# Gate and up weights in pieces of 16 KB: four chunks of 2 MB an expert in place of eight of 1 MB

## The reference

```python
logits = x @ w_router + b_router
top_logit, top_e = top_k(logits, 4)            # 4 of 32 experts for each token
gate = softmax(top_logit)
# for each expert e, for the rows xb routed to it:
gu = xb @ w_gu[e] + b_gu[e]                    # 1024 -> 2048
g, u = split(gu, 2)
g = minimum(g, 7.0); u = clip(u, -7.0, 7.0)
y = ((u + 1.0) * g * sigmoid(1.702 * g)) @ w_down[e] + b_down[e]   # 1024 -> 1024
# y times its gate is summed into the token's row
```

## Time and profile before

| | |
|---|---|
| median of three runs | 1621.77 us |
| the profiled execution's own time | 1619.32 us |
| its span, first to last instruction | 1617.6 us |
| TensorE busy | 1380.0 us, 85% |
| VectorE / ScalarE / GpSimd busy | 25% / 17% / 18% |
| mean rate of the DMAs over the span | 338 GB/s |
| mean granted TensorE clock | 0.913 of full speed |
| chain that ended last, by engine | PE 54%, DMA 34% |
| DMA packets | 110,253 |

### The profile page before, as it was taken

The page is one execution under the profiler, slowest core; times in us unless marked ns, Lnnn a source line. Parts: engine busy times, 40 slices in busy tenths (PEclk is TensorE's granted clock), DMA queues, the critical chain, the costliest instruction groups (busy, mean ns, idle before and its releaser), DMA issues.

```text
span 1617.6 us, 21742 instructions
## 1 busy us (share of the span) xinstructions
PE 1380.0 (85%) x8299; PEld 723.4 (45%) x8299; DVE 398.6 (25%) x759; ACT 282.7 (17%) x496; POOL 293.9 (18%) x288
## 2 busy tenths in 40 slices
PE   4799977788899578999999898899999889986667
PEld 2457753353699444444434443343444334332222
DVE  2358235553122532121111102111111211110103
ACT  1213444343233200111000101100010110000000
POOL 1336523222276010101001110100111010010000
PEclk9899989898999778998999899999989999977777
DMA  9665778776744637999999999999999999999974
GB/s 331 263 259 174 263 276 291 257 288 216 278 157 149 274 131 270 420 420 421 421 421 420 421 420 420 420 415 419 413 420 418 411 420 394 422 419 419 420 294 166
DMA packets 110253, 547.08 MB, mean 338 GB/s; under 512 B 14576, under 2 KB 14696, under 8 KB 57603
## 3 DMA queue, kind: packets, MB, share of 16 engines
q1 hardware_dynamic: 92704, 496.93, 77.0%
q0 software_dynamic: 16544, 45.72, 7.7%
q10 hardware_dynamic: 898, 3.01, 0.5%
HBM read 540.35 MB, written 13.63 MB: 342 GB/s over the span
## 4 chain that ended last, share of the span: by engine, by line
PE 54%; DMA 34%; DVE 5%; ACT 3%; SPq 2%; issue 1%; POOL 1%; ACTq 0%; POOLq 0%; DVEq 0%
PE PS L1583 48%; DMA wide<-in_w_down 19%; DMA wide<-in_w_gu 10%; PE PS L1761 4%; DMA ring<-in_w_in 3%; SPq L533 1%; DMA arena<-in_g_norm 1%; DMA ring<-in_cache_sb_v 1%; POOL WL L619 1%; PE PS L1937 1%; SPq L542 1%; ACT WL L770 0%; PE PS L1956 0%; PE PS L1737 0%; DMA ring<-in_w_ada 0%
## 5 line engine op out<-in xcount | busy, mean ns | idle before, releaser
L1583 PE MATMUL PS<-wide,arena 128*32 128x256 f32 (+2 forms) x4416 | 786.2, 512 | 101.8 <-DMA wide<-in_w_down 52.2
L1583 PEld LDWEIGHTS PS<-wide,arena 128*32 128x32 f32 (+2 forms) x4416 | 314.2, 141 | 546.2 <-issue 384.6
L687 POOL DMA_INDIRECT choice_rows<-arena,rows_of x31 | 31.8, 1026 | 693.7 <-ACT arena L1037 447.5
L619 POOL TENSOR_TENSOR WL<-ring,WL 128x1024 fp32r<-128x1024 f32 x48 | 119.6, 2506 | 132.9 <-ACT WL L770 132.8
L1583 PE MATMUL PS<-WH,WL 128*128 128x288 f32 x768 | 106.0, 299 | 6.3 <-DVEq L1340 3.1
L1583 PEld LDWEIGHTS PS<-WH,WL 128*128 128x128 f32 x768 | 104.2, 190 | 10.2 <-DVEq L1340 3.4
L1494 DVE TENSOR_SCALAR arena<-PS 128x256 f32<-128x256 f32 (+1 forms) x23 | 12.2, 529 | 346.6 <-PE PS L1583 346.6
L1583 PE MATMUL PS<-WL,WH 128*128 128x512 f32 (+1 forms) x288 | 74.4, 421 | 12.2 <-POOL WL L619 6.7
L770 ACT ACTIVATE WL<-ring 128x1024 fp32r<-128x1024 f32 x56 | 58.1, 1055 | 149.7 <-DMA ring<-in_w_in 92.7
L1045 ACT ACTIVATE arena<-arena 128x256 f32<-128x256 f32 (+1 forms) x23 | 11.5, 500 | 367.8 <-DVEq L1495 367.8
L1583 PE MATMUL PS<-ring,arena 128*32 128x512 f32 x256 | 61.4, 656 | 16.8 <-DMA ring<-in_cache_sb_v 13.7
(11 more groups left out here) (280 smaller groups left out, 1120.5 us busy)
## 6 DMA issues: line engine op xcount, KB each, us to landing
wide<-in_w_gu SPq DMA_DIRECT2D x256, 1024.0 KB, 23.5
wide<-in_w_down SPq DMA_DIRECT2D x128, 1024.0 KB, 25.0
ring<-in_w_ada SPq DMA_DIRECT2D x24, 1024.0 KB, 7.1
ring<-in_w_in SPq DMA_DIRECT2D x20, 1024.0 KB, 7.9
ring<-in_cache_sb_k SPq DMA_DIRECT2D x32, 256.0 KB, 4.3
ring<-in_cache_sb_k POOLq DMA_DIRECT2D x32, 256.0 KB, 5.4
ring<-in_cache_sb_v SPq DMA_DIRECT2D x32, 256.0 KB, 4.3
ring<-in_cache_sb_v POOLq DMA_DIRECT2D x32, 256.0 KB, 4.8
```

What stands on the lines that cost most here:

```text
L619: pool.tensor_tensor(low, raw_half(h), high.bitcast(F32), ALU.subtract).then_inc(mix_low, 1)
L687: pool.indirect_dma_start(Y4.rearrange("t (h n) -> (t h) n", h=n), bass.IndirectOffsetOnAxis(ap=rows_of[:, at, 0:1], axis=0), YB[it % 2 if ...
L1583: return T.matmul(out, lhsT, rhs, start=start, stop=stop, skip_group_check=True)
```

## The change

Gate and up weights are cut differently. A partition now takes two neighbouring rows of `w_gu`, a piece of 16 KB, and a chunk is 2 MB and fills two slots: four chunks an expert. Partition p of chunk j holds rows 256j + 2p and 256j + 2p + 1. `gu_big` and `gu_few` wait for a chunk once, go through its two k-tiles, and count it in `chunks_used` once. The contraction's rows are thus dealt out in another order, so `turn_rows` takes every second column out of 256. An expert has 8 chunks in place of 12, and the counts `gu_used` and `dn_used` follow. The down chunks, the slots and their memory stay. Expert 0's gate-up chunk j waits until two ring items more are used, and the tail's read of `choice_rows` waits for chunk i in place of chunk 2i + 1, which is the same slots.

```diff
-EXP_CHUNKS = 12
+WIDE = 12
+EXP_CHUNKS = 8
...
-GU_CHUNKS, DN_CHUNKS = 8, 4
+GU_CHUNKS, DN_CHUNKS = 4, 4
...
-    return (it + 1) * EXP_CHUNKS + DN_CHUNKS + j + 1
+    return (it + 1) * EXP_CHUNKS + GU_CHUNKS - DN_CHUNKS + j + 1
...
-        w_gu = t["w_gu"][0].rearrange("e (k p) n -> e p k n", p=P)
+        w_gu = t["w_gu"][0].rearrange("e (k p two) n -> e p k (two n)", p=P, two=2)
...
+        def gu_slot(j):
+            return wide[:, 2 * j:2 * j + 2, :]
+
+        def dn_slot(j):
+            return wide[:, 2 * GU_CHUNKS + j, :]
...
-                        sp.wait_ge(used, min(NSTREAM - SLOTS + j + 1, NSTREAM))
+                        sp.wait_ge(used, min(NSTREAM - SLOTS + 2 * j + 2, NSTREAM))
...
-                    sp.dma_start(wide[:, j, :], src).then_inc(expert_in[j], 16)
+                    sp.dma_start(gu_slot(j).rearrange("p s n -> p (s n)"), src).then_inc(expert_in[j], 16)
...
-                sp.wait_ge(chunks_used, gu_used(NE - 1, 2 * i + 1))
+                sp.wait_ge(chunks_used, gu_used(NE - 1, i))
...
-                    last = T.transpose(PS[:, 6 + k // 4, (k % 4) * P:(k % 4 + 1) * P], rows[:, k * P:(k + 1) * P], ident)
+                    cols = rows[:, 2 * P * (k // 2):2 * P * (k // 2 + 1)]
+                    last = T.transpose(PS[:, 6 + k // 4, (k % 4) * P:(k % 4 + 1) * P], cols[:, k % 2::2], ident)
...
             def gu_big(it, j):
                 pe.wait_ge(expert_in[j], 16 * (it + 1))
-                w = c3(wide[:, j, :], 512)
-                for q in range(4):
-                    last = mm(PS[:, q, :], XT[:, j, :], w[:, q, :], j == 0, j == DT - 1)
+                for k in range(2 * j, 2 * j + 2):
+                    w = c3(gu_slot(j)[:, k % 2, :], 512)
+                    for q in range(4):
+                        last = mm(PS[:, q, :], XT[:, k, :], w[:, q, :], k == 0, k == DT - 1)
                 last.then_inc(chunks_used, 1)
...
             def gu_few(it, j, n):
                 pe.wait_ge(expert_in[j], 16 * (it + 1))
                 w, per = FF // n, DT // n
-                rows = c3(wide[:, j, :], FF)
-                for gu in range(2):
-                    for g in range(n):
-                        last = mm(PS[rows_of_group(g, n), gu, 0:w], XT[:, j % per, rows_of_group(j // per, n)],
-                                  rows[:, gu, w * g:w * g + w], False, j == DT - 1)
+                for k in range(2 * j, 2 * j + 2):
+                    rows = c3(gu_slot(j)[:, k % 2, :], FF)
+                    for gu in range(2):
+                        for g in range(n):
+                            last = mm(PS[rows_of_group(g, n), gu, 0:w], XT[:, k % per, rows_of_group(k // per, n)],
+                                      rows[:, gu, w * g:w * g + w], False, k == DT - 1)
                 last.then_inc(chunks_used, 1)
```

More of the change, by code:

```diff
@@ L162, in build @@
             XP = early("XP", [P, 4, DT, P], F32R)
-        wide = sb("wide", [P, EXP_CHUNKS, SLOTW])
+        wide = sb("wide", [P, WIDE, SLOTW])
         xT = sb("xT", [P, DT, NTOK])
@@ L541, in load_down @@
                     src = w_dn[bass.ds(e, 1), :, j, :].rearrange("a p n -> (a p) n")
-                    sp.dma_start(wide[:, GU_CHUNKS + j, :], src).then_inc(expert_in[GU_CHUNKS + j], 16)
+                    sp.dma_start(dn_slot(j), src).then_inc(expert_in[GU_CHUNKS + j], 16)
             def load_bias(it, e):
@@ L1960, in gu_big @@
                 pe.wait_ge(expert_in[j], 16 * (it + 1))
-                w = c3(wide[:, j, :], 512)
-                for q in range(4):
-                    last = mm(PS[:, q, :], XT[:, j, :], w[:, q, :], j == 0, j == DT - 1)
+                for k in range(2 * j, 2 * j + 2):
+                    w = c3(gu_slot(j)[:, k % 2, :], 512)
+                    for q in range(4):
+                        last = mm(PS[:, q, :], XT[:, k, :], w[:, q, :], k == 0, k == DT - 1)
                 last.then_inc(chunks_used, 1)
             def down_big(it, j):
-                pe.wait_ge(expert_in[8 + j], 16 * (it + 1))
-                w = c3(wide[:, 8 + j, :], D)
+                pe.wait_ge(expert_in[GU_CHUNKS + j], 16 * (it + 1))
+                w = c3(dn_slot(j), D)
                 for k in range(2 * j, 2 * j + 2):
@@ L1989, in gu_few @@
                 w, per = FF // n, DT // n
-                rows = c3(wide[:, j, :], FF)
-                for gu in range(2):
-                    for g in range(n):
-                        last = mm(PS[rows_of_group(g, n), gu, 0:w], XT[:, j % per, rows_of_group(j // per, n)],
-                                  rows[:, gu, w * g:w * g + w], False, j == DT - 1)
+                for k in range(2 * j, 2 * j + 2):
[4 more added lines that the diff above has]
+                                      rows[:, gu, w * g:w * g + w], False, k == DT - 1)
                 last.then_inc(chunks_used, 1)
             def down_few(it, j, n):
-                pe.wait_ge(expert_in[8 + j], 16 * (it + 1))
+                pe.wait_ge(expert_in[GU_CHUNKS + j], 16 * (it + 1))
                 w, per = D // n, DT // n
-                rows = c3(wide[:, 8 + j, :], D)
+                rows = c3(dn_slot(j), D)
                 for k in range(2 * j, 2 * j + 2):
```

## The result

The changed kernel took 1612.51 us in the median of six runs (1607.85 to 1614.43), the kernel before 1622.04 us (six runs). The ratio is 0.9948 with a 95% interval of 0.9929 to 0.9967: 8.4 us less (5.4 to 11.5). A second comparison gave 0.9959 (0.9945 to 0.9973). Together the change is worth about half a per cent.

What follows compares the result with a forecast made beforehand. The expert stage was taken as bound by the slowest DMA engine's time for its weight pieces. Terms -9.2 + 1.4 + 0.3 = -7.5 us gave 1611.8 for the profiled execution, 1614.3 for the median; range 1605 to 1623.

Steps and rivals of the forecast that it cites:

- the saving in the stream: Expert weight queue: 32 pieces and four semaphore writes fewer save 0.308 us an expert, 9.2 us over 30 experts.
- What bounds the stage: Expert stage: the slowest DMA engine's time for its share of 12 MB sets the pace, 31.31 us an expert.
- The price of a piece: Gate-up loads: one 16 KB piece beats two of 8 KB by 8.5 ns, middle of 7.1 and 9.9; bounds 0 and 16.3.
- the prediction's own correction: Piece times from the DMA view: divided by the queues' summed share, as packets overlap; 315.5 became 311.4 ns under load.
- B: Weight stream: the whole raw difference, 16.3 ns, is real because load disturbs packets, not bytes; -15.0 us, 1606.8; chance 0.18.
- The start of the stream: Expert 2's first chunk waits for two k-tiles of expert 1 in place of one: 1.4 us lost.
- Expert 0 and the release in pairs: Expert 0's later first chunk and slots freed one k-tile later both cost nothing, covered by slack and 19 to 28 us landings.
- Rival C: Big experts: slots freed in pairs let the slowest engine run dry, 27.4 us lost, 1641.7; chance 0.07.
- Strided transposes: Row transposes before the first expert: weight loads of 208 against 155 ns, eight on the chain, 0.3 us lost.
- The end: End of the expert stage: down chunks still end the chain, so 2 MB gate-up chunks cost nothing there.
- Rival A: Weight stream: a 16 KB piece costs two of 8 KB, so +0.6 us, 1622.4; chance 0.20 with gains up to half.
- the Trainium skill: Weight queue: its 2.0 us per DMA is not seen between queued chunks; joining pieces pays only to 256 bytes, so no gain.

Runs made afterwards that it cites:

- bias_twice: Changed kernel with each expert's 8 KB bias row fetched a second time into an unused partition of the same tile; 1624.37 us, ratio 1.0022 to the kernel before.
- bias_spread_2: Changed kernel with the bias row fetched by two DMAs of alternate 64-float runs, spread over the engines; 1614.22 us, ratio 0.9965 to the kernel before.
- gu_8k: Changed kernel with the same 2 MB gate-up chunks, each fetched as two 8 KB pieces a partition; 1620.64 us, ratio 1.0014 to the kernel before.

## Why the prediction was right, point by point

The forecast was 1614.3 us, 7.5 us less; measured were 8.4 us less in the first comparison (9.5 between the medians) and 0.0041 of 1620.6, 6.6 us, in the second. The forecast, not a rival, came true. That it came this near owes something to luck: the saving in the stream was put 2 us too high, and the two comparisons lie 1.8 us apart.

*What bounds the stage.* The pace of the slowest engine. bias_twice shows it: 8 KB on one engine cost 10 us, some sixteen times what a mean rate would make of them. The semaphore writes show the last engine 9.5 us behind the next by expert 30, and the bias row on it. The prediction left open what makes that engine slow. I then took the bias row for it, and bias_spread_2 showed that taking the row away is not enough; the reason is open.

*The price of a piece.* 8.5 ns for each piece less was put down, between 0 and 16.3. The runs gave 8 ns from 16 to 8 KB, 9 from 8 to 4 KB, 9 on the down weights. So the price was right to within 1 ns, but the way to it was not. The packets' own durations in the trace, 640 to 1540 us, are 315.4 ns in the mean for a piece of 8 KB before and 620.9 for one of 16 KB after. With the prediction's own correction (over 1.004) the latter is 618.4, where it had 612.9 to 615.7: load added more to a piece of 16 KB than it allowed for. And B's 16.3 ns came from setting pieces under load against tail pieces without it. The raw difference, both under load, is 2 x 315.4 - 620.9 = 9.9 ns, and the next packet of an engine begins 3 to 4 ns before the end of the one before, so each piece less also gives up one such overlap. The prediction's correction would leave 2 x 311.4 - 618.4 = 4.4 ns. The 8.5 was the middle of two options that both missed the load, and its fit with 8 to 9 is partly luck.

The sum of the term was too high, 0.308 us an expert against 0.23 to 0.26 measured. Of this 0.036 were four semaphore writes, of which gu_8k shows nothing (31.33 against 31.31), and the rest is no more than the spread of the paces. 30 x 0.24 = 7.2 us in place of 9.2.

*The start of the stream.* 1.4 us was put down, 1.5 to 1.7 measured between TensorE's first gate-up matmul of expert 1 and SyncE's issue. TensorE's first k-tiles of expert 1 run at a granted clock of 0.50 (626.93 to 628.90 us) and 0.53 (up to 630.70), about the lower level of 1.2 GHz, and those behind them at 1.00, so one k-tile more costs more there than the mean of 1.06 us. The first issue came at 630.77 and not at 629.3; 1.1 us of this come from the matmuls, which began later.

*Expert 0 and the release in pairs.* Nothing and nothing. Here a number of the text was wrong, though its conclusion held. I had doubled SyncE's longest wait of 3.2 us to 6.4. SyncE's waits of the changed kernel in 640 to 1540 us (total, times, longest), against the earlier trace rows:

```profile
SPq L540 <- PE PS L1590: 476.1, 116, 10.9
```

The longest is 10.9 us. The reserve of 18 to 28 us covers that too, and 23.4 us is still the median landing time of gate-up chunks in that stretch. Rival C would have needed a reserve under 4.9.

*Strided transposes.* The weight load of L1945 (L1937 before) went from 155 to 208 ns, the figure of L1956, as expected. The eight transposes on the chain took 1.96 us against 1.94 before, so the 0.3 us were not there.

*The end.* From the landing of the last chunk to the end of the span it is 35.8 us in both (1576.87 to 1612.7, 1581.85 to 1617.6).

*The sum.* -7.2 + 1.6 = -5.6 us by the paces, and the profiled executions differ by 4.9. The measured 6.6 to 8.4 us are 1 to 3 us more, and the intervals of the ratios, 2.3 us either side and more, allow that. Part of it is the start: the changed kernel's profiled execution reached expert 1's gate-up matmuls 1.1 us later. From there to the end of the span it is 991.8 us before and 985.8 and 985.0 in the two profiles of the changed kernel, 6.0 to 6.8 less.

*Rival A and the Trainium skill.* Rival A wanted 31.3 us an expert; it was 31.08. Making the pieces 16 KB paid 8 ns for each piece less, which is 1.3% of the time of a 16 KB piece and just above the noise of the kernel.

The prediction used two sections more widely than they are meant. The Trainium skill, "DMA: Bandwidth & Descriptors", section "Why small descriptors are slow", calls packetization, the joining of consecutive descriptors into one packet, worth it only up to 256 bytes. This change makes the piece itself larger, so it does not follow from there that it gains nothing, and no run here tests packetization. The Trainium skill, "DMA: Bandwidth & Descriptors", section "Anatomy of one DMA", gives its fit of 2.0 us plus bytes / 436e3 for DMAs on GpSimd's path, while the weights here are issued by SyncE. That four DMAs fewer don't save 4 x 2 us stands on gu_8k: 31.33 us an expert against 31.31.

## What to carry to other kernels

When a stage is bound by its weight stream, count pieces for each engine: here a piece cost some 8 to 9 ns beside its bytes, between 4 and 16 KB, and larger chunks with fewer semaphore writes brought nothing without larger pieces. Ask which engine is last rather than what the mean rate is: a small transfer added to the last engine cost some sixteen times its share of the bytes. The reverse does not follow, as the spread row gained nothing. Before you infer from paces what the engines do, look at the semaphore writes of one chunk, which say how far apart they are. To see half a per cent, compare the pace between two landings far apart in the trace, since the span of one profile shifts by more than the effect through work that has nothing to do with it.

## What the runs showed of the hardware that I had not expected

- One 8 KB row more an expert, in one piece, made the stage slower by 0.37 us an expert, a little more than the 0.31 us that such a piece takes; the first row, spread over the engines, gained nothing.
- The engines drift apart. In the changed kernel one of them is 1.30 us behind the next at expert 5 and 9.51 us at expert 30, and chunks land by that one.
- A DMA written as 16 contiguous runs of 512 bytes went out as one piece of 8 KB; alternate runs stayed apart.
- A matmul of a four-way expert that reads every fourth float of its 256 columns took 564 ns in the mean over gate, up and down, against 437 with contiguous columns; gate and up are two thirds of these matmuls. The mean granted clock was 0.938 there and 0.923 in the other.
- Four DMAs and four semaphore writes an engine less for each expert had no worth that can be measured: 31.33 us an expert in gu_8k against 31.31 before.
